# Reordered loads, stores and sample copies, and three elementwise products moved from GpSimd to VectorE, in a one-core fp32 transformer block

## The reference

```
fq, fk, fv, ff, dq, dk, dv, iq, ik, iw = split(x @ w_in)
fox = softmax(fq @ fk.T / 8 + forget bias, causal) @ fv            # 8 heads of 64
idx = top_k(sum_h iw_h * relu(iq_h @ ik.T), 256)                   # admissible keys of each query
dsa = softmax(dq @ dk[idx].T / 8) @ dv[idx]                        # 8 heads, 2 key/value heads
h   = layer_norm(alpha * x + concat(fox, dsa) @ w_out)
f   = (silu(h @ w_gate) * (h @ w_up)) @ w_down                     # d_ff = 2816
y   = layer_norm(alpha * h + f)
```

## Time and profile before

| | |
|---|---|
| time, median of 3 runs | 1430.89 us (1428.64 to 1433.03) |
| profiled execution | 1433.38 us, its span 1431.6 us |
| busy, share of the span | PE 1372.8 us (96%), PEld 1221.6 (85%), DVE 986.7 (69%), ACT 695.2 (49%), POOL 531.6 (37%) |
| granted TensorE clock, mean | 0.992 of full |
| DMA | 192.27 MB, mean 134 GB/s |

### The profile page before, as it was taken

One profiled execution on the slowest core, in us unless ns is written; L12 is line 12 of the kernel. 1 busy time (PEld: TensorE's weight loads), 2 busy tenths in 40 slices (PEclk: granted clock), 3 DMA queues, 4 the chain that ended last, 5 costly groups with the idle time before them and its releaser, 6 DMA issues.

```text
span 1431.6 us, 23837 instructions
## 1 busy us (share of the span) xinstructions
PE 1372.8 (96%) x8985; PEld 1221.6 (85%) x8985; DVE 986.7 (69%) x1820; ACT 695.2 (49%) x1268; POOL 531.6 (37%) x571
## 2 busy tenths in 40 slices
PE   7989999999999899899999999999999998999997
PEld 7869989987777677687889999999999996778886
DVE  4489899778784989847775455555645656846488
ACT  5579889548684788710242223333223234524331
POOL 3632435622231022324465555555555551010011
PEclk9999999999999999999999999999999999999999
DMA  7102322358834211421124443454344449847554
GB/s 237 55 13 62 109 66 77 84 140 223 200 104 121 59 54 38 148 93 44 44 91 150 159 148 127 154 170 164 119 138 153 147 160 358 286 140 247 167 168 155
DMA packets 142738, 192.27 MB, mean 134 GB/s; under 512 B 21416, under 2 KB 99208, under 8 KB 142624
## 3 DMA queue, kind: packets, MB, share of 16 engines
q1 hardware_dynamic: 142624, 190.75, 42.2%
HBM read 134.59 MB, written 46.15 MB: 126 GB/s over the span
## 4 chain that ended last, share of the span: by engine, by line
PE 38%; POOL 8%; DVE 5%; issue 3%; ACT 1%; DMA 1%; POOLq 0%; DVEq 0%; SPq 0%; ACTq 0%
PE ffn L2676 21%; PE ffn L2191 6%; POOL w_lo L2957 5%; POOL gated L2966 3%; PE ffn L2776 3%; PE ffn L2777 3%; PE ffn L2778 3%; DVE down_lo L3041 2%; ACT w_hi L2832 1%; DMA down_raw<-in_w_down 1%; DVE rows L3175 1%; PE ffn L2650 1%; PE ffn L2795 0%; PE ffn L2793 0%; DVE ln_stats L2079 0%
## 5 line engine op out<-in xcount | busy, mean ns | idle before, releaser
L2957 POOL TENSOR_TENSOR w_lo<-w_S,w_hi 128x512 fp32r<-128x512 f32 x88 | 119.7, 1360 | 107.5 <-ACT w_hi L2832 107.5
L2676 PE MATMUL ffn<-h_T_hi,w_hi 128*128 128x264 f32 x704 | 145.6, 287 | 2.3 <-POOL w_lo L2957 2.1
L2676 PE MATMUL ffn<-h_T_lo,w_hi 128*128 128x264 f32 x704 | 143.7, 285 | 0.0
L2932 ACT CAST down_hi<-down_raw 128x1024 fp32r<-128x1024 f32 (+1 forms) x77 | 89.5, 1173 | 109.9 <-DMA down_raw<-down_w 46.5
L2676 PE MATMUL ffn<-h_T_hi,w_lo 128*128 128x264 f32 x704 | 142.8, 283 | 0.0
L2095 POOL TENSOR_TENSOR ln_rstd<-ln_var_eps,ln_power 128x1 f32<-128x1 f32 (+1 forms) x18 | 29.4, 1632 | 277.1 <-DVE ln_var_eps L2075 144.8
L3041 DVE TENSOR_TENSOR down_lo<-down_raw,down_hi 128x1024 fp32r<-128x1024 f32 (+1 forms) x77 | 105.0, 1387 | 35.0 <-ACT down_hi L2932 34.7
L2776 PE MATMUL ffn<-down_hi 128*128 128x512 f32 x308 | 121.4, 394 | 6.1 <-DVE down_lo L3041 6.1
L2832 ACT CAST w_hi<-w_S 128x512 fp32r<-128x512 f32 x88 | 54.7, 621 | 143.3 <-PE ffn L2676 141.9
L2777 PE MATMUL ffn<-down_lo,down_hi 128*128 128x512 f32 x308 | 121.0, 393 | 0.0
L2778 PE MATMUL ffn<-down_hi,down_lo 128*128 128x512 f32 x308 | 121.0, 393 | 0.0
(11 more groups left out here) (416 smaller groups left out, 3948.3 us busy)
## 6 DMA issues: line engine op xcount, KB each, us to landing
down_raw<-down_a SPq DMA_DIRECT2D x77, 256.0 KB, 3.5
gate_raw<-in_w_gate SPq DMA_DIRECT2D x11, 1024.0 KB, 6.7
up_raw<-in_w_up SPq DMA_DIRECT2D x11, 1024.0 KB, 6.4
down_t<-in_w_down SPq DMA_DIRECT2D x44, 256.0 KB, 4.1
down_w<-down_t SPq DMA_DIRECT2D x22, 512.0 KB, 3.4
down_raw<-in_w_down SPq DMA_DIRECT2D x22, 512.0 KB, 5.7
down_raw<-down_w SPq DMA_DIRECT2D x44, 256.0 KB, 4.0
down_a<-down_s SPq DMA_DIRECT2D x10, 1024.0 KB, 4.1
```

Source lines behind the costliest of these rows:

```text
L2676: mm = nc.tensor.matmul(pp[:, bank[to] + ch, 0:PIECE], l, x[name][:, k, ch * PIECE:(ch + 1) * PIECE], start=opens and k == 0 and i == 0, s ...
L2932: nc.scalar.copy(hs[:, 0:n], raws[s % RAWS][:, 0:n]).then_inc(hi_done, 1)
L2957: nc.gpsimd.tensor_tensor(w_lo[n % 2][:, :, :], weight(m, SCHEME[q][0]), f32(w_hi[n % 2][:, :, :]), ALU.subtract).then_inc(w_lo_done, 1)
```

## The change

- A: in `project`, the load of group g + 2 is issued behind the third store of group g instead of ahead of its first, for groups 2 to 7.
- B: in `loads`, the copies of head 6 go from batch 6 to batch 7, those of head 7 from batch 7 to batch 9.
- C: in the first half block the lows of the samples' rest stand behind the lows of T3 tiles 2 and 3 instead of ahead of them, with the second sum between; the fifth product waits for the samples' lows.
- D: in the down stage, the kept rows come back in three pieces at other places (tiles 6 and 7 in the last half block, tile 4 behind load 2, tile 5 behind load 9), and the last `store_s` goes behind load 10. The last sample copy, its pair and the last activation sums come one step later.
- E: `times` moves to VectorE, behind each of the three sums of an odd half block, and `keep_samples` stands one product later on ACT.

```diff
@@ -429,10 +429,12 @@
             n_out = 0
             for g in range(NG):
                 name = GROUPS[g][0]
-                if g + 2 < NG:
+                if g < 2:
                     load_w(g + 2)
                 for u in OF_GROUP[g]:
                     _, t, ch = UNITS[u]
+                    if u == OF_GROUP[g][3] and 2 <= g < NG - 2:
+                        load_w(g + 2)
                     if GROUPS[g][2]:
                         s = STAGED.index(u) % NSTAGE
                         if name == "fk":
@@ -1614,9 +1616,9 @@
                 stack_head(sp, 3)
                 sp.wait_ge(c_done, 4)
                 sp.dma_start(d["bias_s"][:, 0:PAST], bias_s[:, :]).then_inc(bias_stored, 16)
-            if b in (2, 6):
-                stack_head(sp, b + 2 if b == 2 else 6)
-            elif b in (3, 7):
+            if b in (2, 7):
+                stack_head(sp, 4 if b == 2 else 6)
+            elif b in (3, 9):
                 stack_head(sp, 5 if b == 3 else 7)
             if b % 4 == 2 and b // 4 + 2 < 4:
                 sp.wait_ge(s["v_lo_done"], 2 * (b // 4) + 2)
@@ -2346,7 +2348,7 @@
 COPIED = EARLY + [("B21", 1), ("B21", 2), ("T1", 0), ("T1", 1), ("T1", 2), ("T2", 0), ("S", "T1"), ("B11", 3), ("T1", 3),
                   ("S", "T2"), ("T2", 1), ("B21", 3), ("T2", 2), ("T2", 3), ("S", "rest")] + PAIRED
 LOWERED = EARLY + [("T1", 0), ("T1", 1), ("B21", 1), ("B11", 3), ("T1", 2), ("S", "T1"), ("T2", 0), ("B21", 2), ("T1", 3), ("B21", 3),
-                   ("S", "T2"), ("T2", 1), ("T2", 2), ("T2", 3)] + PAIRED[:4] + [("S", "rest")] + PAIRED[4:]
+                   ("S", "T2"), ("T2", 1), ("T2", 2), ("T2", 3)] + PAIRED[:6] + [("S", "rest")] + PAIRED[6:]
 BANKS = {("B11", 0): 2, ("B11", 1): 3, ("B11", 2): 4, ("B21", 0): 5, ("B21", 1): 3, ("B21", 2): 4, ("T1", 0): 2, ("T1", 1): 5,
          ("T1", 2): 6, ("T2", 0): 7, ("B11", 3): 0, ("T1", 3): 2, ("T2", 1): 6, ("B21", 3): 3, ("T2", 2): 7, ("T2", 3): 6}
 BANKS.update({(x, j): 7 - j % 2 for x in ("T3", "B22", "T4") for j in range(4)})
@@ -2592,6 +2594,8 @@
                     store_s(m // 2 - 1)
                 if m == NM - 1:
                     load_step(0)
+                    sp.wait_ge(s_stored, s_stored_at + 16 * (NB - 1))
+                    sp.dma_start(y[:, 6:NT, :], d["kept"][2:4].rearrange("t p n -> p t n")).then_inc(rows_moved, 16)
                 if m:
                     store_t(m - 1)
                 if m + 2 < NM:
@@ -2600,21 +2604,25 @@
                     load_t(0)
                 if m + 1 < NM:
                     load_t(m + 1)
-            for s in range(1, 5):
-                load_step(s)
+            load_step(1)
+            load_step(2)
+            sp.wait_ge(t_stored, t_stored_at + 16 * (NM - 1))
+            sp.dma_start(y[:, 4, :], d["kept"][0]).then_inc(rows_moved, 16)
+            load_step(3)
+            load_step(4)
             store_t(NM - 1)
             load_step(5)
             load_step(6)
             store_a(NB - 1)
             load_step(7)
             load_step(8)
-            sp.wait_ge(s_stored, s_stored_at + 16 * (NB - 1))
-            sp.dma_start(y[:, 6:NT, :], d["kept"][2:4].rearrange("t p n -> p t n")).then_inc(rows_moved, 16)
-            store_s(NB - 1)
             load_step(9)
             sp.wait_ge(t_stored, t_stored_at + 16 * NM)
-            sp.dma_start(y[:, 4:6, :], d["kept"][0:2].rearrange("t p n -> p t n")).then_inc(rows_moved, 16)
-            for s in range(10, STEPS):
+            sp.dma_start(y[:, 5, :], d["kept"][1]).then_inc(rows_moved, 16)
+            load_step(10)
+            store_s(NB - 1)
+            load_step(11)
+            for s in range(12, STEPS):
                 load_step(s)
                 if s == S_OUT + 2:
                     sp.dma_start(gain[:, :], d["ln2_g"].partition_broadcast(P)).then_inc(ln_loaded, 16)
@@ -2716,7 +2724,7 @@
             transposes("T4", 0)
             transposes("T4", 1)
             pe.wait_ge(w_lo_done, 5)
-            pe.wait_ge(h_lo, lowered_at("T3", 3))
+            pe.wait_ge(h_lo, lowered_at("S", "rest"))
             pe.wait_ge(u2_done, 1)
             products(4, 4, ks=range(KH // 2))
             transposes("T4", 2)
@@ -2907,7 +2915,7 @@
                     if n + 2 < NP:
                         split(n + 2)
                     if m % 2 == 0:
-                        if q == 0:
+                        if q == 1:
                             keep_samples(m // 2 - 1)
                         elif q == 4:
                             silu(m // 2, "C11", 0)
@@ -2933,9 +2941,9 @@
 
             for s in range(STEPS):
                 split_step(s)
-                if s == 2:
+                if s == 3:
                     keep_samples(NB - 1)
-                elif s == 3:
+                elif s == 4:
                     act.wait_ge(s_kept, NB)
                     act.wait_ge(c12_done, NM)
                     nc.scalar.copy(a_pair[:, :, 0:NEW], a_s[:, :, :]).then_inc(pair_hi, 1)
@@ -2956,14 +2964,6 @@
                 pool.wait_ge(w_hi_done, n + 1)
                 nc.gpsimd.tensor_tensor(w_lo[n % 2][:, :, :], weight(m, SCHEME[q][0]), f32(w_hi[n % 2][:, :, :]),
                                         ALU.subtract).then_inc(w_lo_done, 1)
-
-            def last_of(b):
-                times(b, "C12", 2)
-
-            def times(b, name, i):
-                pool.wait_ge({"C22": c22_done, "C21": c21_done, "C12": c12_done}[name], 2 * b + 2)
-                pool.wait_ge(silu_done, 4 * b + 4)
-                nc.gpsimd.tensor_tensor(of_gated(name), of_gated(name), other[:, :], ALU.mult).then_inc(times_up, 1)
 
             def differences(name, j):
                 t = TILE_ORDER[j]
@@ -3008,14 +3008,6 @@
                     b = m // 2
                     if n + 2 < NP:
                         split(n + 2)
-                    if m % 2 and q == 5:
-                        times(b, "C22", 0)
-                    elif m % 2 and q == 6:
-                        times(b, "C21", 1)
-                    elif m % 2 == 0 and m and q == 0:
-                        last_of(b - 1)
-
-            last_of(NB - 1)
             for n, t in enumerate([NT] + LN_ROUND[0]):
                 norm.root(pool, t, TILES[t][2], n)
             for n, t in enumerate(LN_ROUND[1]):
@@ -3093,6 +3085,11 @@
                         last = nc.vector.tensor_tensor(s_cols(lo[name]), s_sum(name), f32(s_cols(hi[name])), ALU.subtract)
                 last.then_inc(h_lo, 1)
 
+            def times(b, name):
+                dve.wait_ge({"C22": c22_done, "C21": c21_done, "C12": c12_done}[name], 2 * b + 2)
+                dve.wait_ge(silu_done, 4 * b + 4)
+                nc.vector.tensor_tensor(of_gated(name), of_gated(name), other[:, :], ALU.mult).then_inc(times_up, 1)
+
             def second_sum(m):
                 dve.wait_ge(p1_copied, m + 1)
                 dve.wait_ge(product_done, m * NQ + at_of(m, 1) + 1)
@@ -3113,9 +3110,9 @@
                     mix_weights(0, ("S2",))
                 elif x == ("T3", 1):
                     mix_weights(0, ("S3",))
+                elif x == ("T3", 3):
+                    second_sum(0)
                 elif x == ("S", "rest"):
-                    second_sum(0)
-                elif x == ("T3", 3):
                     mix_weights(0, ("S4",))
             for m in range(NM):
                 up, b, n = m % 2, m // 2, m * NQ
@@ -3141,6 +3138,8 @@
                     dve.wait_ge(times_up, 3 * b)
                 nc.vector.tensor_tensor(two(other[:, :] if up else of_gated("C22")), area("Z"), two(u3[:, :]), ALU.add)\
                     .then_inc(c22_done, 1)
+                if up:
+                    times(b, "C22")
                 if m == NM - 1:
                     lower_step(0)
                 elif m:
@@ -3150,6 +3149,8 @@
                     dve.wait_ge(times_up, 3 * b + 1)
                 nc.vector.tensor_tensor(two(other[:, :] if up else of_gated("C21")), two(u3[:, :]), area("V"), ALU.subtract)\
                     .then_inc(c21_done, 1)
+                if up:
+                    times(b, "C21")
                 if m + 1 < NM:
                     mix_weights(m + 1, ("S4",) if m else ("S1", "S2", "S3", "S4"))
                 if m == NM - 1:
@@ -3160,11 +3161,13 @@
                     dve.wait_ge(times_up, 3 * b + 2)
                 nc.vector.tensor_tensor(two(other[:, :] if up else of_gated("C12")), area("Z"), two(u2[:, :]), ALU.add)\
                     .then_inc(c12_done, 1)
+                if up:
+                    times(b, "C12")
 
             def add(p, i):
                 dve.wait_ge(tile_done, 4 * p + i + 1)
                 if p == 0:
-                    dve.wait_ge(rows_moved, 48)
+                    dve.wait_ge(rows_moved, 64)
                 for k, (t0, half) in enumerate(ADDED[p]):
                     o, new = y[:, t0 + i, 512 * half:512 * half + 512], pp[:, DOWN[p][2] + i, :]
                     before = added_before(p, (t0, half))
@@ -3204,11 +3207,11 @@
 
```

(4 more changed lines are left out.)

## The result

The changed kernel takes 1420.63 us (median of 9 runs) beside 1430.89 us: 0.9941 of before, 95% interval 0.9920 to 0.9962, so 8.4 us saved (5.4 to 11.4) where 18.6 were forecast. The time lies inside the stated range of 1408 to 1422, but the change is worth 8.4 us and not 18.6, so the prediction was wrong in size. The profiled execution took 1427.49 us (span 1425.7), at the slow end of the nine.

The account below looks back on a forecast made before the run. TensorE (PE) was taken as the bound, with long gaps paid twice through the clock. 5.0 + 4.9 - 0.7 + 6.4 + 3.0 = 18.6 us off gave 1412 us against the 1430.89 median, range 1408 to 1422.

Parts of the forecast that it names:

- A: Projections: with three stores ahead of the weight load, PE's stage-copy waits (3.4 us) and slow clock (1.6) go; gain 5.0 us.
- B: Key bias wanted near 377 us: without copies ahead it lands sooner; 2.45 us gap plus 2.5 clock, gain 4.9, lower bound 2.5.
- C: First half block: PE's 1.49 us gap at 735 moves to the T4 transposes, some 2 us; 0.7 us lost, at worst 2.5.
- D: Start of the down projection: waits of 1.6 and 3.5 us and 1.3 of clock go; gain 6.4 us, lower bound 1.6.
- E: Gate and up half-block pairs: products leave GpSimd, pair period falls from 41.37 us; gain 3.0 us, bounds 0 and 4.9.
- no VectorE wait over 1.5 us for a key bias: Sign expected in the profile after: VectorE never stands longer than 1.5 us for a key bias.
- the 1.6 us at the first steps: Down projection, until 1194.56: PE's wait behind ACT's sample copy and fourth weight split goes; 1.6 us of D's gain.
- the long wait: Down projection, until 1218.08: PE's 3.52 us wait for loads of steps 9 to 11 goes, with 1.3 us of clock.
- 0.2 us per pair for w_lo behind the C12 product: Gate and up stage: the C12 product on VectorE would push GpSimd's w_lo by 0.2 us, a loss kept in E.
- the first rival: The port eats E: VectorE's products hold w_lo back as often as GpSimd's did; E gives 0, 1415 us; chance 0.2.
- the case that A and B are half hidden and E is worth nothing: Third rival: ranking holds PE and the bias lands late, 4.9 us less; with E at 0 too 1420 us; chance 0.1.
- the long wait, A and B half hidden and C at its worst: Rival "within 0.3%": the long wait stays, A and B are half hidden, C costs 2.5; 1427 us, chance 0.04.

## Why the prediction was wrong, step by step

- **B failed.** Forecast: 4.9 us gained, since what is queued behind the moved copies "are softmax scales, which only GpSimd wants, and the sample's past keys, wanted at the end of the stage". That asked who wants the late transfers, and not who comes next in the queue behind them: the bias of head 6. In the new order SP issues the six copies from 365.99 on and the past loads right behind them, from 375.00 to 379.98; the last of these lands at 388.64. The bias, issued at 381.90, stands behind them and shares the engines with head 7's copies; it lands at 393.76, where VectorE wanted it at 393.78 - 7.30 = 386.48. Before, the past loads went out at nearly the same time (from 376.21 on), but the bias came 4.4 us later (386.28), and head 7's copies had gone out at 369.45. The bytes agree: from the bias of head 5 at 365.63 through head 7's copies 5.8 MB are issued (0.5 + 1.5 + two softmax scales of 0.25 + 2.0 of past loads + 0.5 + 0.75), and at the mean 217 GB/s of the page of this stretch they need some 27 us, so until 392 (an estimate, with the rate of this very stretch). The loss is 6.5 us on average. Shown by part B undone and by the past loads moved.
- **B's gain was also sized on one profile.** 2.45 us of gap and 2.5 us of clock were the dearest of five: the stretch without the moved copies is worth 0 to -3.8 us, so with them -5.1 means 2.8 us gained, near the lower bound. Net, B loses 3.7 us (2.8 - 6.5) instead of winning 4.9.
- **A held:** 5.0 forecast, 5.4 found against the profile of before (4.9 against the mean of three); no wait for a stage copy and a clock of 1.00 behind it. The sign asked for a clock of 1.00 through the projections; it fell at 98, which no part touches. The sign of no VectorE wait over 1.5 us for a key bias failed twice, with the 7.30 us and with 2.77 us for head 3's at 343.19.
- **C had the right mechanism, and the wrong size:** the gap was forecast at the T4 transposes, some 2 us instead of 1.49, and is 1.86 us; the term was 0.7 and measures 2.0 (+2.4 against +0.4), within the bound of 2.5. The clock falls behind the gap in three of nine profiles. A late up load (PE idle 1.46 to 4.05 us in four of the nine) is part of the mean; one of 0.79 us came with C undone too, so it looks like scatter of the DMA, which was not tried by itself.
- **D held:** 6.4 forecast, 6.0 found (6.2 less the 0.2 without). One term is smaller than booked: the 1.6 us at the first steps go with part E as well, and the long wait is dearer by its clock (0.50 over 4 us with D undone). In exchange PE waits 0.83 us for VectorE's row additions at 1228, which it didn't before.
- **E was under-sized:** 3.0 forecast, 4.9 found (-4.9 against 0.0), the upper bound. I had kept 0.2 us per pair for w_lo behind the C12 product; it doesn't come, PE waits for no w_lo in the steady pairs. The products do suffer, as the tile answer of after shows (ns min/median/max):

```profile
L3091 DVE TENSOR_TENSOR gated<-gated,other x33: 707/1071/1141, 770.7 to 1187.9; 128x528 f32<-128x528 f32 x33
```

0.71 us alone and 1.07 in the median, and VectorE's busy time rises from 200 to 216 us of 356. The collision is there and lies in idle time. The Trainium skill (SBUF — State Buffer, "Who interferes with whom") has two such instructions contend for one shared port, with which this trace agrees, though the products that overlap a w_lo by 0.5 us lose less than that (0.36 us in the median); that E would be worth nothing by it, as the first rival had it, was refuted by the ten waits that came back with E undone.
- **The sum by the measured terms:** 4.9 - 3.7 - 2.0 + 6.0 + 4.9 = 10.1 us, beside 8.4 (5.4 to 11.4) measured. The forecast's 18.6 less B's 8.6 of error is 10.0: without that one term the forecast would have stood inside the interval, in part by luck, since C was 1.3 us too high and E 1.9 too low.
- **The range** held the time by luck: its upper end was set for the case that A and B are half hidden and E is worth nothing, and that isn't what happened. One rival was added up wrongly, too: the long wait, A and B half hidden and C at its worst leave 2.5 + 2.5 - 2.5 + 1.6 + 3.0 = 7.1 us, so 1424 and not 1427, which would need E at nothing as well.

## What to carry to other kernels

Before you move transfers in a queue, find the next transfer that anybody waits for and add up all bytes issued up to it and right behind it, those between the moved ones too, and divide by the rate that the windows show: who wants the moved ones is only half the question. Here 5.8 MB at 0.217 MB/us gave the landing within 2 us; the moved copies, the past loads, this bias and head 7's copies alone (4.8 MB at 0.24) would have given 386, and no stall. Size a stall that hangs on a DMA's landing from more than one profile, because here the same one measured 0.8 to 2.5 us and another 1.5 to 7.2. When a reordering leaves a gap in another place, look where the late engine next stands idle, and put the work there: two tiles further on the same operations cost nothing.

## What the runs showed of the hardware

The 512 KB load of the bias of head 6 landed in 3.9 us with B undone, in 7.2 to 12.1 us with it, and in 5.0 to 5.5 us with B and the past loads behind it; the eight loads of this kind in the kernel after took between 3.5 and 11.9 us. And the same gap of 3.1 us at 98 us let the granted clock fall to the 1.2 GHz level in 15 of 17 profiles and not in two (before, and part B undone); that is worth 1.2 to 2.7 us, up to a third of what the whole change gained, and no part touches anything ahead of it.
